# Expert tiles of 96 slots shared in column groups, with two overflow units in a thirteenth tile

## The chip, the cores and the metric

One core of one Trainium2 chip runs the whole program. The metric is the device time of one execution in microseconds; for a kernel it is the median of its runs. Inputs, weights and outputs are float32 in HBM.

## The reference, cut to what matters

The program is one inference step of a decoder of two layers, for 512 prompt tokens and 32 sample tokens (8 sequences of 4). Each layer has a projection, a gated recurrence, differential attention (the sample tokens against a paged cache), an output projection and then a mixture of experts, which alone is changed here:

```python
def hier_moe(xn, w_r1, b_r1, w_r2, b_r2, w_gate, w_up, w_down):
    xt = xn.reshape(-1, d)                                # 544 tokens of width 1024
    ... top-1 group of 4, top-2 of the 4 experts in it, weights from the two softmaxes
    y = jnp.zeros_like(xt)
    for e in range(N_EXPERTS):                            # 16
        h = jax.nn.silu(xt @ w_gate[e]) * (xt @ w_up[e])  # width 512
        y = y + (h * gates[:, e:e + 1]) @ w_down[e]
    return y.reshape(b, t, d)
```

So each token goes to exactly two experts: 1088 assignments over 16 experts in a layer, 68 for an expert on average.

## The kernel before, in words

Everything is written out by hand: each engine has its own list of instructions, in a fixed order, with waits on semaphores between them. A helper `link` on VectorE makes each instruction wait for the one before it.

**Routing.** After the output projection, `logits` (L868) and `route` (L1538) find each token's two experts. A matmul with a triangular matrix counts each assignment's position in its expert. `psel` holds, per token and expert, the slot or −1. An expert has P = 128 slots, which are the 128 rows of its tile.

**One expert, one tile.** For expert e, `sel_build` (L1625) compares the slots with 0..127, `slot_ids` (L878) multiplies that selection with the token number and the gate value, and `ids_out` (L1632) brings both to SBUF. POOL gathers the tokens' rows from HBM by an indirect DMA into `xe` (L1889). `x_turn` (L888) transposes them with eight matmuls against the identity, and VectorE scales them on the way to `xeT` (`x_out`, L1618). `gate_up` (L899) is 2 × 8 matmuls with 128 tokens as the stationary operand and 512 columns of weights moving. ScalarE takes the silu (L1249), VectorE multiplies gate value, silu and up (L1752). `h_turn` (L912) transposes, and `down` (L921) is 2 × 4 matmuls. ScalarE copies the two halves of the result (L1255, L1257) and POOL stores the tile in `y_scratch` (`y_store`, L1831).

**The order on TensorE** (L1017 to L1026) is, for each e: `gate_up(e)`, `x_turn(e+1)`, `down(e-1)`, `slot_ids(e+2)`, `h_turn(e)`. The other engines follow the same order.

**Weights.** SP loads them in the order of `weight_plan` (L122), gate, up and down of each expert, 2 MB each, in six slots of SBUF in turns. `load_w` (L450) waits until the last matmul on the slot's former content is done (`last_use`, L403). Before the experts start, six loads are out.

**Overflow.** Assignments beyond slot 127 of an expert go to extra tiles. `extra_plan` (L1578) counts them and finds each one's expert; after the sixteen tiles, `extra_tiles` (L419) runs as many extra tiles as a register says, all engines in lockstep: the tile's weights are loaded by an address from a register into slots 2, 3 and 4 (L527), then ids, gather, transposes, matmuls and the store follow each other with nothing beside them.

**Results.** `result_rows` (L1600) works out for each token the two rows of `y_scratch` that hold its results. POOL gathers these (L1911) and VectorE adds them to the residual (L1798); the next layer or the final norm follows.

**Column groups.** Some parts of the kernel already use matmuls narrower than 128 columns of the stationary operand. In `sample_chunks` (L577) the 32 sample tokens are the stationary operand, and successive chunks go to output partitions 0, 32, 64 and 96 in turns; `quad_scores` (L664), `quad_values` (L699) and `level` (L797) do the like. `level` for b = 64 (L824) has 64 columns, always at output partitions 0 to 63.

```python
                for c in range(DC):
                    a = 32 * (c % 4)
                    x = mm(o[a:a + NS, :], xT[:, c, S:TOK], w[:, c, :], start=(c < 4), stop=(c >= 4))
```

Of the kernel before, what the change touches and what calls it, by code (L numbers as in the profile page):

```python
# [25 lines left out]
P = 128  # L26
# [12 lines left out]
YROWS = NE * P  # L39
# [3 lines left out]
MAXX = 2 * TOK // P  # L43
AT0 = 8

XV = {"sel": 7, "ids": 10, "x": 12, "all": 13}
# [21 lines left out]
def constants():  # L68
# [3 lines left out]
    for i in range(PT):  # L72
# [20 lines left out]
        "ebase": np.broadcast_to(P * np.arange(NE)[None, :], (P, NE)),  # L93
# [27 lines left out]

def weight_plan():  # L122
    plan = []
    for l in range(L):
        plan += [("in", l, j, (2, 3, 0, 1)[j % 4]) for j in range(7)]
        plan += [("out", l, n, 1 - n) for n in range(2)]
        for e in range(NE):
            for k in range(3):
                plan.append((("gate", "up", "down")[k], l, e, (2, 3, 4, 5, 0, 1)[(3 * e + k) % 6]))
    where, count = {}, [0] * 6  # L130
# [9 lines left out]
def build(nc, t_in, t_out):  # L140
# [4 lines left out]
    with ctx:  # L145
# [28 lines left out]
        def wslot(s):  # L174
            return w_a[:, 4096 * s:4096 * (s + 1)] if s < 4 else h_a[:, 4096 * (s - 4):4096 * (s - 3)]
# [70 lines left out]
        smalls = sb("smalls", 2148)  # L246
# [61 lines left out]
        tg = small("id_and_gate", (NT, NE, 2))  # L308
        rk = small("y_rows_f", (2, NT))
        rki = small("y_rows", (2, NT), U32)  # L310
        idx = small("slot_tokens", (NE,), U32)
        gate = small("slot_gates", (NE,))

        rx = m_a[:, 5144:5160]
        cntx = shaped(m_a[:, 5096:5144], (3, NE))
        ohx = small("extra_expert", (MAXX, NE))
        ohx2 = shaped(m_a[:, 4968:5096], (MAXX, NE))
# [5 lines left out]
        tgx = small("extra_id_and_gate", (NT, 2))  # L323
        xid = small("extra_tokens", (1,), U32)
        xidf = small("extra_tokens_f", (1,))
        xgt = small("extra_gates", (1,))
# [3 lines left out]
        y_d = nc.dram_tensor("y_scratch", [YROWS + MAXX * P, D], F32, kind="Internal").ap()  # L330
# [4 lines left out]
        wl = [sem(f"w_loaded{i}") for i in range(6)]  # L335
        kl = [sem(f"x_tile_then_k_page_loaded{i}") for i in range(NK)]
        vl = [sem(f"v_quad_loaded{i}") for i in range(NV)]
        prep_a, prep_v = sem("lb_exps"), sem("prep_steps")
# [64 lines left out]
        def last_use(key):  # L403

            what, l, j = key
            if what == "in":
                return (tp_ps, 12 * l + PT * (j + 1)) if j < 3 else (fp_ps, 32 * l + 8 * (j - 2))
            if what == "out":
                return wo_ps, 10 * l + 2 * (PT - 1) + j + 1
            if what == "down":  # L410
                return y_ps, 2 * (NE * l + j) + 2
            return gu_ps, 2 * (NE * l + j) + (1 if what == "gate" else 2)
# [6 lines left out]
        def extra_tiles(eng, ready, body):  # L419

            eng.wait_ge(rk_ok, ready)
            n = eng.value_load(nxi[0:1, 0:1], min_val=0, max_val=MAXX)
            with eng.If(0 < n):
                with eng.Fori(0, MAXX) as t:
                    with eng.If(t < n):
                        body(t)

                        eng.sem_inc(passed, 1)

# [8 lines left out]
        def _(sp):  # L438
            with nc.allow_non_contiguous_dma(reason="small parameter columns"):
# [10 lines left out]
                def load_w(n):  # L450
# [32 lines left out]
                for l in range(L):  # L483
# [36 lines left out]
                    for q in range(3 * NE):  # L520
# [6 lines left out]
                    def extra(t):  # L527
                        e = sp.value_load(exi[0:1, bass.ds(t, 1)], min_val=0, max_val=NE - 1)
# [5 lines left out]
                    sp.wait_ge(*last_use(("down", l, NE - 2)))  # L534
# [6 lines left out]
        def _(pe):  # L541
# [336 lines left out]
            def slot_ids(l, e):  # L878

                E_ = l * NE + e  # L880
                pe.wait_ge(sel_ok, E_ + 1)
                if e >= 1:
                    pe.wait_ge(id_ok, E_)
# [4 lines left out]
            def x_turn(l, e):  # L888
                E_ = l * NE + e
                pe.wait_ge(xe_in[e % 2], 16 * (l * (NE // 2) + e // 2 + 1))  # L890
                if E_ >= 1:
                    pe.wait_ge(xe_ok, 2 * E_)
                for j in range(2):
                    for c in range(4):
                        k = 4 * j + c
                        x = tr(bank[j][:, c * P:(c + 1) * P], xe[e % 2][:, k * P:(k + 1) * P], ident)  # L896
                    x.then_inc(xe_ps, 1)

            def gate_up(l, e):  # L899

                E_ = l * NE + e
                pe.wait_ge(xe_ok, 2 * E_ + 2)
                if E_ >= 1:
                    pe.wait_ge(hg_ok, E_)
# [7 lines left out]
            def h_turn(l, e):  # L912
                E_ = l * NE + e
                pe.wait_ge(hg_ok, E_ + 1)
                if E_ >= 1:
                    pe.wait_ge(ht_ok, E_)
# [4 lines left out]
            def down(l, e):  # L921
                E_ = l * NE + e
                pe.wait_ge(ht_ok, E_ + 1)
                wwait(pe, ("down", l, e))
                w = weights(("down", l, e), 4)
                for n in range(2):
                    if E_ >= 1:
                        pe.wait_ge(y_ok, 2 * E_ - 1 + n)
                    for c in range(4):
                        x = mm(bank[5 + n][:, :], hT[e % 2][:, c, :], w[:, c, n * WB:(n + 1) * WB], start=(c == 0), stop=(c == 3))  # L930
# [3 lines left out]
            for l in range(L):  # L934
                if l:
                    pe.wait_ge(y_ok, 2 * NE * l)
# [80 lines left out]
                for e in range(NE):  # L1017
                    gate_up(l, e)
                    if e + 1 < NE:
                        x_turn(l, e + 1)  # L1020
                    if e >= 1:
                        down(l, e - 1)
                    if e + 2 < NE:
                        slot_ids(l, e + 2)
                    h_turn(l, e)
                down(l, NE - 1)  # L1026

                def extra(t):
                    V_, A_ = t * XV["all"], t * XA["y"]
                    pe.wait_ge(xv[l], V_ + XV["sel"])  # L1030
                    for i in range(NT):
                        x = mm(bank[7][:, 0:2], sel[:, i, :], tgx[:, i, :], start=(i == 0), stop=(i == NT - 1))
# [26 lines left out]
                pe.wait_ge(y_ok, 2 * NE * (l + 1))  # L1059
# [4 lines left out]
        def _(act):  # L1064
# [70 lines left out]
            for l in range(L):  # L1135
                norm_roots(2 * l)
                if l == 0:

                    act.wait_ge(prep_v, 1)
                    A(lbe[:, :, :], lbe[:, :, :], ACT.Exp).then_inc(prep_a, 1)  # L1140
                    A(dls[:, :, :], dls[:, :, :], ACT.Exp).then_inc(prep_a, 1)
# [28 lines left out]
                if l == 0:  # L1170

                    act.wait_ge(zero_st, 16 * MAXX)
# [70 lines left out]
                for e in range(NE + 1):  # L1243
                    if e < NE:
                        E_ = l * NE + e
                        act.wait_ge(gu_ps, 2 * E_ + 1)
                        if E_ >= 2:
                            act.wait_ge(hg_ok, E_ - 1)
                        A(silu[e % 2], bank[2][:, :], ACT.Silu).then_inc(si_ok, 1)  # L1249
                    if e >= 1:  # L1250
                        E_ = l * NE + e - 1
                        act.wait_ge(y_ps, 2 * E_ + 1)
                        if E_ >= 2:
                            act.wait_ge(y_st[(e - 1) % 2], 16 * (E_ // 2))
                        A(yt[(e - 1) % 2][:, 0:WB], bank[5][:, :], ACT.Copy).then_inc(y_ok, 1)  # L1255
                        act.wait_ge(y_ps, 2 * E_ + 2)
# [697 lines left out]
```

## Time and profile before

| | us |
|---|---|
| median of 3 runs | 2113.6 (2112.17 to 2118.08) |
| profiled execution, its own time | 2108.49 |
| its span, first to last instruction | 2106.8 |
| stage of the sixteen expert tiles, layer 0 | 630 to 998 |
| the same, layer 1 | 1637 to 2013 |
| extra tile, layer 1 (none in layer 0) | 2014 to 2066 |

The span is what the profile shows; the execution's own time is 1.7 us longer. PE is TensorE's matmuls, PEld its weight loads, DVE is VectorE, ACT ScalarE. A record of TensorE is one pass; a float32 matmul leaves two records, a transpose one. The shape 128*64 128x512 of a record is the stationary operand's rows and columns, then the moving operand. A record's duration is longer than its share of the engine, since records overlap; what counts is the distance between starts. "PEclk" is the granted share of TensorE's full clock.

### The profile page before, as it was taken

How to read it: one execution, taken by the hardware profiler on the slowest of the kernel's cores; microseconds unless marked ns; L12 is line 12 of the kernel's file. 1: busy time of each engine (PE TensorE's matmuls, PEld its weight loads, DVE VectorE, ACT ScalarE, POOL GpSimd, SP SyncE). 2: the span in 40 equal slices, each digit the busy share in tenths (PEclk: the TensorE clock that was granted, in tenths of full speed). 3: DMA queues.
4: the chain of work that ended last, by engine and by line, in shares of the span. 5: the costliest groups of instructions: out<-in, count | busy, mean ns of one | idle time of the engine just before them, and what ended most of it. 6: DMA issues, size and time to landing. Idle time of an engine off the chain costs nothing. (4 is left out here: it accounts for less than half of the span.)

```text
span 2106.8 us, 30190 instructions
## 1 busy us (share of the span) xinstructions
PE 1867.4 (89%) x11372; PEld 1094.4 (52%) x11372; DVE 595.9 (28%) x1635; ACT 505.9 (24%) x1072; POOL 181.6 (9%) x236
## 2 busy tenths in 40 slices
PE   7999989787979999999599998988888899999970
PEld 3467767455454554454245776654544444454430
DVE  3215365421141111110420554553213311111103
ACT  2123246455110111011111332654511011111001
POOL 1000022100000010000200001311000010010002
PEclk9999989999969999999799998999998899999985
DMA  8321059897535989986522104888962389988744
GB/s 283 127 75 42 1 190 308 276 310 279 216 112 179 328 300 328 329 303 238 213 91 72 41 21 137 269 293 284 347 239 103 110 315 331 329 300 327 263 150 147
DMA packets 209281, 453.23 MB, mean 215 GB/s; under 512 B 23217, under 2 KB 23218, under 8 KB 209138
## 3 DMA queue, kind: packets, MB, share of 16 engines
q1 hardware_dynamic: 189986, 383.52, 52.5%
q0 software_dynamic: 19152, 67.77, 8.5%
q8 instruction: 93, 1.52, 0.3%
q14 instruction: 50, 0.41, 0.1%
HBM read 413.89 MB, written 37.36 MB: 214 GB/s over the span
## 5 line engine op out<-in xcount | busy, mean ns | idle before, releaser
L909 PE MATMUL bank<-wslots,heads 128*128 128x512 f32 x768 | 339.0, 598 | 2.7 <-DVE heads L1622 2.7
L620 PE MATMUL bank<-xT,wslots 128*128 128x272 f32 x1024 | 241.8, 393 | 1.5 <-ACT heads L1169 0.8
L909 PEld LDWEIGHTS bank<-wslots,heads 128*128 128x128 f32 x768 | 146.1, 192 | 182.0 <-issue 178.4
L620 PEld LDWEIGHTS bank<-xT,wslots 128*128 128x128 f32 x1024 | 191.6, 190 | 40.7 <-issue 3.2
L661 PE MATMUL bank<-cst,wslots 128*128 128x128 f32 x1024 | 164.3, 287 | 12.9 <-DMA wslots<-in_cache_k 7.5
L574 PE MATMUL bank<-wslots,xT 128*128 128x512 f32 x384 | 169.3, 595 | 0.0
L1752 DVE SCALAR_TENSOR_TENSOR temps<-temps,smalls,bank 128x512 f32<-128x512 f32 x32 | 23.9, 747 | 432.1 <-PE bank L909 432.1
L661 PEld LDWEIGHTS bank<-cst,wslots 128*128 128x128 f32 x1024 | 115.5, 144 | 38.9 <-issue 22.8
L861 PE MATMUL bank<-wslots,xT 128*128 128x512 f32 x256 | 115.1, 610 | 3.8 <-DVE xT L1521 3.8
L574 PEld LDWEIGHTS bank<-wslots,xT 128*128 128x128 f32 x384 | 71.3, 190 | 87.5 <-issue 87.3
L930 PE MATMUL bank<-wslots,temps 128*128 128x512 f32 x256 | 112.7, 593 | 1.5 <-ACT temps L1261 1.5
L909 PE MATMUL bank<-hgrn,heads 128*128 128x512 f32 x256 | 112.7, 593 | 0.1
L930 PE MATMUL bank<-hgrn,temps 128*128 128x512 f32 x256 | 112.5, 592 | 0.0
L1219 ACT ACTIVATE heads<-bank 128x512 f32<-128x512 f32 x128 | 74.9, 595 | 110.1 <-PE bank L661 109.8
L1219 ACT ACTIVATE wslots<-bank 128x512 f32<-128x512 f32 x128 | 75.9, 593 | 96.6 <-PE bank L661 88.3
L1255 ACT ACTIVATE heads<-bank 128x512 f32<-128x512 f32 x32 | 19.1, 597 | 323.2 <-PE bank L930 323.2
L1469 DVE TENSOR_SCALAR_CACHE_REDUCE heads<-bank 128x512 f32<-128x512 f32 x64 | 44.2, 691 | 155.8 <-PE bank L672 132.8
L861 PEld LDWEIGHTS bank<-wslots,xT 128*128 128x128 f32 x256 | 49.6, 196 | 66.5 <-issue 62.3
L711 PE MATMUL bank<-wslots,heads 128*32 128x128 f32 x2048 | 75.1, 292 | 6.9 <-ACT heads L1234 6.9
L711 PEld LDWEIGHTS bank<-wslots,heads 128*32 128x32 f32 x2048 | 60.0, 118 | 36.0 <-ACT heads L1234 21.2
L1249 ACT ACTIVATE temps<-bank 128x512 f32<-128x512 f32 x32 | 19.1, 597 | 238.4 <-PE bank L909 238.4
L930 PEld LDWEIGHTS bank<-wslots,temps 128*128 128x128 f32 x256 | 47.4, 190 | 55.5 <-issue 53.6
(332 smaller groups left out, 2078.4 us busy)
## 6 DMA issues: line engine op xcount, KB each, us to landing
wslots<-in_w_up SPq DMA_DIRECT2D x33, 2048.0 KB, 21.1
wslots<-in_cache_k SPq DMA_DIRECT2D x256, 256.0 KB, 4.4
wslots<-in_cache_v SPq DMA_DIRECT2D x256, 256.0 KB, 4.5
wslots<-in_w_gate SPq DMA_DIRECT2D x17, 2048.0 KB, 16.3
hgrn<-in_w_down SPq DMA_DIRECT2D x17, 2048.0 KB, 10.7
hgrn<-in_w_gate SPq DMA_DIRECT2D x16, 2048.0 KB, 16.5
wslots<-in_w_down SPq DMA_DIRECT2D x16, 2048.0 KB, 10.6
wslots<-in_w_in SPq DMA_DIRECT2D x14, 2048.0 KB, 10.0
```

Of the source, the lines that this page charges most:

```text
L574: x = mm(bank[2 + m % 2][:, :], xT[:, c, tok(i)], w[:, c, :], start=(c == 0), stop=(c == DC - 1))
L620: x = mm(bank[6 + g % 2][:, 0:HALF], w[:, c, h * P:(h + 1) * P], xT[:, c, half * HALF:(half + 1) * HALF], start=(c == 0), stop=(c == DC - 1))
L661: x = tr(bank[s % 2][:, h * P:(h + 1) * P], kpage[s % NK][:, h, :], ident)
L711: x = mm(bank[5][32 * h:32 * h + 32, 0:HD], ptq[par][:, j, 32 * h:32 * h + 32], vquad[v % NV][:, j, h, :], start=(q == 0 and j == 0), stop ...
L861: x = mm(bank[2 + s][:, :], oT[:, c, tok(i)], w[:, c, :], start=(c == 0), stop=(c == DC - 1))
L909: x = mm(bank[2 + k][:, :], xeT[e % 2][:, c, :], w[:, c, :], start=(c == 0), stop=(c == DC - 1))
L930: x = mm(bank[5 + n][:, :], hT[e % 2][:, c, :], w[:, c, n * WB:(n + 1) * WB], start=(c == 0), stop=(c == 3))
L1219: A(ktb[s // 4 % 2][:, s % 4].rearrange("p h n -> p (h n)"), bank[s % 2][:, :], ACT.Copy).then_inc(kt_ok, 1)
L1249: A(silu[e % 2], bank[2][:, :], ACT.Silu).then_inc(si_ok, 1)
L1255: A(yt[(e - 1) % 2][:, 0:WB], bank[5][:, :], ACT.Copy).then_inc(y_ok, 1)
L1469: tell(V.tensor_scalar(scr[G_ % 6], bank[2][:, :], 1.0, None, ALU.mult, ALU.max, accum_out=mx5[:, g % 4:g % 4 + 1]), sq_ok)
L1752: link(V.scalar_tensor_tensor(hgt, silu[e % 2], gate[:, e:e + 1], bank[3][:, :], ALU.mult, ALU.mult), hg_ok)
```

## The change

Each expert has 96 slots instead of 128, so four experts share three tiles of 128 rows. The rows of a tile that belong to different experts are multiplied with different weights: a chunk of `gate_up` or `down` is now two or three matmuls, each with 32 or 64 columns of the stationary operand and its own output partitions. Assignments beyond slot 95 form units of 64 rows. The first two units of a layer have a thirteenth tile, whose weights SP loads by register after the others; further units would go through the serial loop. The gate value is no longer multiplied into the tile but when the results are added. The weights have a seventh slot in `xT`.

```diff
-YROWS = NE * P
+CAP, XCAP = 96, 64
+TILES = NE * CAP // P + 1
+YROWS = NE * CAP
-MAXX = 2 * TOK // P
+MAXX = 15
+ZT = 8
...
+def tile_parts(t):
+    if t == TILES - 1:
+        return [(NE, 0, XCAP), (NE + 1, XCAP, P)]
+    parts = []
+    for e in range(NE):
+        lo, hi = max(CAP * e - P * t, 0), min(CAP * (e + 1) - P * t, P)
+        while lo < hi:
+            z = min(hi, lo + 64 if lo % 64 == 0 and hi - lo >= 64 else lo + 32)
+            parts.append((e, lo, z))
+            lo = z
+    return parts
+
+def tiles_of(e):
+    return [t for t in range(TILES) if any(e == x for x, _, _ in tile_parts(t))]
 def weight_plan():
+    need = []
+    for e in range(NE + 2):
+        t = tiles_of(e)
+        need += [(3 * t[0], e, "gate", 3 * t[-1]), (3 * t[0] + 1, e, "up", 3 * t[-1] + 1), (3 * t[0] + 5, e, "down", 3 * t[-1] + 5)]
+    need.sort(key=lambda x: x[:2])
...
-        for e in range(NE):
-            for k in range(3):
-                plan.append((("gate", "up", "down")[k], l, e, (2, 3, 4, 5, 0, 1)[(3 * e + k) % 6]))
+        free = {s: k - 7 for k, s in enumerate((2, 3, 4, 5, 0, 1, 6))}
+        for _, e, what, last in need:
+            slot = min(free, key=lambda s: free[s])
+            free[slot] = last
+            plan.append((what, l, e, slot))
...
+                    elif j >= NE:
+                        sp.wait_ge(rk_ok, l + 1)
+                        e = sp.value_load(exi[0:1, j - NE:j - NE + 1], min_val=0, max_val=NE - 1)
+                        src = t_in["w_" + what][l, bass.ds(e, 1)].rearrange("o k n -> (o k) n")
...
-                    for q in range(3 * NE):
+                    for q in range(3 * (NE + 2)):
+                        if q == 6:
+                            sp.wait_ge(lg_ps, NT * (l + 1))
...
-                    x = mm(bank[7][:, 0:2], sels[e % 2][:, i, :], tg[:, i, e, :], start=(i == 0), stop=(i == NT - 1))
+                    x = mm(bank[7][:, 0:1], sels[T_ % 2][:, i, :], tokid[:, i:i + 1], start=(i == 0), stop=(i == NT - 1))
...
+                parts = tile_parts(t)
                 for k, what in enumerate(("gate", "up")):
-                    wwait(pe, (what, l, e))
-                    w = weights((what, l, e), DC)
+                    for e, _, _ in parts:
+                        wwait(pe, (what, l, e))
                     for c in range(DC):
-                        x = mm(bank[2 + k][:, :], xeT[e % 2][:, c, :], w[:, c, :], start=(c == 0), stop=(c == DC - 1))
+                        for e, a, z in parts:
+                            x = mm(bank[2 + k][a:z, :], xeT[T_ % 2][:, c, a:z], weights((what, l, e), DC)[:, c, :], start=(c == 0), stop=(c == DC - 1))
                     x.then_inc(gu_ps, 1)
...
                     for c in range(4):
-                        x = mm(bank[5 + n][:, :], hT[e % 2][:, c, :], w[:, c, n * WB:(n + 1) * WB], start=(c == 0), stop=(c == 3))
+                        for e, a, z in parts:
+                            x = mm(bank[5 + n][a:z, :], hT[T_ % 2][:, c, a:z], weights(("down", l, e), 4)[:, c, n * WB:(n + 1) * WB],
+                                   start=(c == 0), stop=(c == 3))
...
-                b16 = lambda a: a.unsqueeze(2).to_broadcast([P, NT, NE])
-                t16 = r16.rearrange("p i g j -> p i (g j)")
-                link(V.tensor_tensor(t16, f1, b16(r1[:, 6]), ALU.mult))
-                link(V.tensor_tensor(psel[:, :, :], f2, b16(r1[:, 7]), ALU.mult))
-                V.tensor_copy(tg[:, :, :, 0], b16(con("tokid")))
-                link(V.tensor_tensor(tg[:, :, :, 1], t16, psel[:, :, :], ALU.add))
...
-                link(V.tensor_scalar(cntx[:, 0], cnt, float(P), None, ALU.is_gt))
-                for k in range(2, NT):
-                    link(V.scalar_tensor_tensor(cntx[:, 0], cnt, float(P * k), cntx[:, 0], ALU.is_gt, ALU.add))
+                link(V.tensor_scalar(cntx[:, 0], cnt, float(CAP), None, ALU.is_gt))
+                for k in range(1, -(-(TOK - CAP) // XCAP)):
+                    link(V.scalar_tensor_tensor(cntx[:, 0], cnt, float(CAP + XCAP * k), cntx[:, 0], ALU.is_gt, ALU.add))
...
-                link(V.tensor_tensor(sels[e % 2], iota.unsqueeze(1).to_broadcast([P, NT, P]), psel[:, :, e].unsqueeze(2).to_broadcast([P, NT, P]),
-                                ALU.is_equal), sel_ok)
+                for e in range(NE):
+                    base = CAP * e - P * t
+                    lo, hi = max(base, 0), min(base + CAP, P)
+                    if lo < hi:
+                        x = V.scalar_tensor_tensor(dst[:, :, lo:hi], iota[:, lo:hi].unsqueeze(1).to_broadcast([P, NT, hi - lo]), float(-base),
+                                                   psel[:, :, e].unsqueeze(2).to_broadcast([P, NT, hi - lo]), ALU.add, ALU.is_equal)
+                link(x, sel_ok)
...
-                V.tensor_copy(idx[:, e:e + 1], bank[7][:, 0:1])
-                link(V.tensor_copy(gate[:, e:e + 1], bank[7][:, 1:2]), id_ok)
+                link(V.tensor_copy(idx[:, t:t + 1], bank[7][:, 0:1]), id_ok)
...
-                    link(V.scalar_tensor_tensor(hgt, silu[e % 2], gate[:, e:e + 1], bank[3][:, :], ALU.mult, ALU.mult), hg_ok)
+                    link(V.tensor_tensor(hgt, silu[T_ % 2], bank[3][:, :], ALU.mult), hg_ok)
...
-                        link(V.tensor_tensor(hid[0:r, i, :], hid[0:r, i, :], yg[2 * i + k][0:r, :], ALU.add), moe_add)
+                        link(V.scalar_tensor_tensor(hid[0:r, i, :], yg[2 * i + k][0:r, :], r1[0:r, 6 + k, i:i + 1], hid[0:r, i, :], ALU.mult, ALU.add), moe_add)
```

The parts of the tiles are, in turns: 64 and 32 columns of one expert and 32 of the next; 64 of one and 64 of the next; 32 of one and 32 and 64 of the next. The thirteenth tile is 64 of unit 0 and 64 of unit 1. For this tile `sel_build` first works out the slots of the two units with three small operations each. The loops over experts on POOL, ScalarE and VectorE run over the thirteen tiles in the same order as before, and `extra_tiles` counts from the third unit.

## Rows read from the trace of the kernel before

**Rows 1.** The page, part 1: busy us, share of the span, instructions.
```profile
PE 1867.4 (89%) x11372; PEld 1094.4 (52%) x11372; DVE 595.9 (28%) x1635; ACT 505.9 (24%) x1072; POOL 181.6 (9%) x236
```

**Rows 2.** Windows: stretch, length, busy PE, PEld, DVE, ACT, POOL, clock, DMA share, GB/s.
```profile
630.00:998.00 368.00, 367.15 (x1092) 180.99 (x1092) 51.79 (x110) 37.39 (x63) 25.63 (x29) 0.99 0.79 285
1637.00:2013.00 376.00, 370.83 (x1108) 183.99 (x1108) 59.26 (x137) 37.46 (x64) 27.70 (x31) 0.98 0.79 282
...
694.70:704.70 10.00, 10.00 (x27) 4.50 (x25) 0.89 (x2) 1.19 (x2) 1.45 (x2) 1.00 0.96 344
704.70:714.70 10.00, 10.00 (x31) 4.93 (x30) 2.13 (x3) 0.60 (x1) 0.00 (x0) 1.00 1.03 385
```

**Rows 3.** Timeline (start, us, engine, line), one expert of layer 0: TensorE, then SP.
```profile
694.76 7.03 PE L909 MATMUL bank<-hgrn,heads 128*128 128x512 f32 x16
701.63 7.03 PE L909 MATMUL bank<-wslots,heads 128*128 128x512 f32 x16
...
693.45 0.37 SPq L463 DMA_DIRECT2D wslots<-in_w_down  x1
...
716.43 0.37 SPq L463 DMA_DIRECT2D hgrn<-in_w_down  x1
```

**Rows 4.** Timeline of POOL after the last expert tile, layer 0, then layer 1.
```profile
999.50 0.53 POOL L1834 DMA_DIRECT2D y_scratch<-heads  x1 [7.45 <-ACT heads L1257]
1003.22 0.98 POOL L1911 DMA_INDIRECT hgrn<-y_scratch,smalls  x1 [3.20 <-DMA y_scratch<-heads]
...
2013.98 0.53 POOL L1834 DMA_DIRECT2D y_scratch<-heads  x1 [7.90 <-ACT heads L1257]
...
2065.84 0.99 POOL L1911 DMA_INDIRECT hgrn<-y_scratch,smalls  x1 [6.62 <-issue]
```

**Rows 5.** DMA issues: count, KB each, median us from issue to landing.
```profile
wslots<-in_w_up SPq DMA_DIRECT2D x33, 2048.0 KB, 21.1
...
y_scratch<-heads POOLq DMA_DIRECT2D x33, 512.0 KB, 8.7
```

**Rows 6.** Timeline of TensorE in short windows: the 32-wide matmuls of L581.
```profile
45.38 1.07 PE L581 MATMUL bank<-wslots,xT 128*32 128x512 f32 x8
...
45.84 1.04 PE L581 MATMUL bank<-wslots,xT 128*32 128x512 f32 x8
...
46.70 0.61 PE L581 MATMUL bank<-wslots,xT 128*32 128x512 f32 x4
47.24 1.13 PE L574 MATMUL bank<-wslots,xT 128*128 128x512 f32 x2
```

**Rows 7.** The same: from 32-wide to 32-wide work, and from 32-wide to 64-wide.
```profile
300.76 1.07 PE L672 MATMUL bank<-heads,smalls 128*32 128x512 f32 x8
301.65 0.19 PE L818 MATMUL bank<-hgrn 128*32 128x32 f32 x1
...
332.46 1.06 PE L672 MATMUL bank<-heads,smalls 128*32 128x512 f32 x8
333.45 0.27 PE L824 MATMUL bank<-hgrn 128*64 128x64 f32 x1
```

**Rows 8.** Two lines' matmuls: duration ns min/median/max, first and last start.
```profile
L581 PE MATMUL bank<-wslots,xT x160: 592/592/617, 45.4 to 1592.4; 128*32 128x512 f32 x160
...
L824 PE MATMUL bank<-hgrn x64: 222/222/271, 333.5 to 1353.2; 128*64 128x64 f32 x64
```

**Rows 9.** Timeline of VectorE ahead of the first expert tile, layer 0.
```profile
624.48 0.59 DVE L1583 SCALAR_TENSOR_TENSOR temps<-bank,temps 128x16 f32<-128x16 f32 x3
...
625.54 0.29 DVE L1588 TENSOR_TENSOR smalls<-cst,temps 128x128 f32<-128x128 f32 x1
...
628.62 1.42 DVE L1622 TENSOR_TENSOR heads<-bank,smalls 128x512 f32<-128x512 f32 x2
```

**Rows 10.** Groups of VectorE by form: busy us, mean ns, idle before them.
```profile
L1752 DVE SCALAR_TENSOR_TENSOR temps<-temps,smalls,bank 128x512 f32<-128x512 f32 x32 | 23.9, 747 | 432.1 <-PE bank L909 432.1
...
L1803 DVE SCALAR_TENSOR_TENSOR hid<-hid,smalls,xT 128x1024 f32<-128x1024 f32 x4 | 5.1, 1284 | 0.1
```

More of the change, by code:

```diff
@@ L42 @@
 HALF = TOK // 2
-MAXX = 2 * TOK // P
+MAXX = 15
+ZT = 8
 AT0 = 8
-XV = {"sel": 7, "ids": 10, "x": 12, "all": 13}
+XV = {"sel": 4, "ids": 5, "x": 7, "all": 8}
 XP = {"ids": 1, "x": 2, "gate_up": 3, "h": 4, "all": 5}
@@ L307, in build @@
         psel = small("slot_or_none", (NT, NE))
[L308 removed]
         rk = small("y_rows_f", (2, NT))
         rki = small("y_rows", (2, NT), U32)
[L311 to L315, printed above, removed]
+        idx = small("slot_tokens", (TILES,), U32)
+        rx = m_a[:, 5272:5288]
+        cntx = shaped(m_a[:, 5224:5272], (3, NE))
         ohx = small("extra_expert", (MAXX, NE))
[L317 removed]
+        ohx2 = shaped(m_a[:, 4968:4968 + MAXX * NE], (MAXX, NE))
         kx = small("extra_first_slot", (MAXX,))
@@ L409, in last_use @@
                 return wo_ps, 10 * l + 2 * (PT - 1) + j + 1
+            t = TILES * l + tiles_of(j)[-1]
             if what == "down":
-                return y_ps, 2 * (NE * l + j) + 2
-            return gu_ps, 2 * (NE * l + j) + (1 if what == "gate" else 2)
+                return y_ps, 2 * t + 2
+            return gu_ps, 2 * t + (1 if what == "gate" else 2)
         def projected(l, n):
@@ L919, in h_turn, with down @@
                 x.then_inc(ht_ps, 1)
[L921 to L925, printed above, removed]
+            def down(l, t):
+                T_ = l * TILES + t
+                pe.wait_ge(ht_ok, T_ + 1)
+                parts = tile_parts(t)
+                for e, _, _ in parts:
+                    wwait(pe, ("down", l, e))
                 for n in range(2):
-                    if E_ >= 1:
-                        pe.wait_ge(y_ok, 2 * E_ - 1 + n)
+                    if T_ >= 1:
+                        pe.wait_ge(y_ok, 2 * T_ - 1 + n)
                     for c in range(4):
-                        x = mm(bank[5 + n][:, :], hT[e % 2][:, c, :], w[:, c, n * WB:(n + 1) * WB], start=(c == 0), stop=(c == 3))
+                        for e, a, z in parts:
+                            x = mm(bank[5 + n][a:z, :], hT[T_ % 2][:, c, a:z], weights(("down", l, e), 4)[:, c, n * WB:(n + 1) * WB],
+                                   start=(c == 0), stop=(c == 3))
                     x.then_inc(y_ps, 1)
@@ L1016, in _ @@
                 x_turn(l, 0)
[L1017 to L1026, printed above, removed]
+                for t in range(TILES):
+                    gate_up(l, t)
+                    if t + 1 < TILES:
+                        x_turn(l, t + 1)
+                    if t >= 1:
+                        down(l, t - 1)
+                    if t + 2 < TILES:
+                        slot_ids(l, t + 2)
+                    h_turn(l, t)
+                down(l, TILES - 1)
                 def extra(t):
@@ new lines, in sel_build @@
+            def sel_build(l, t):
+                T_ = l * TILES + t
+                if T_ >= 2:
+                    dve.wait_ge(id_ps, T_ - 1)
+                dst = sels[T_ % 2]
+                if t == TILES - 1:
+                    for u in range(2):
+                        extra_slots(ohx[:, u:u + 1, :].to_broadcast([P, NT, NE]), kx[:, u:u + 1].to_broadcast([P, NT]))
+                        x = V.tensor_tensor(dst[:, :, XCAP * u:XCAP * (u + 1)], iota[:, 0:XCAP].unsqueeze(1).to_broadcast([P, NT, XCAP]),
+                                            psx[:, :].unsqueeze(2).to_broadcast([P, NT, XCAP]), ALU.is_equal)
+                        if u == 0:
+                            link(x)
+                    link(x, sel_ok)
+                    return
+                for e in range(NE):
[4 more added lines that the diff above has]
+                                                   psel[:, :, e].unsqueeze(2).to_broadcast([P, NT, hi - lo]), ALU.add, ALU.is_equal)
+                link(x, sel_ok)
```

231 lines of the change are left out of this document (114 added, 117 removed).

## The prediction

> **What bounds the kernel now.** I first took the page: TensorE is busy 1867 of 2107 us [rows 1]. The windows over the two expert stages say more: 367 of 368 us busy in layer 0, 371 of 376 in layer 1, at a granted clock of 0.99 and 0.98 [rows 2]. So the expert stage is bounded by what TensorE issues, and its time can be counted. The timeline of one expert gives the count [rows 3]: gate, up and down are 24 matmuls, and a float32 matmul leaves two records, so 48; 16 of them take from 694.76 to 701.63, 0.429 us each, 20.6 us in all. Eight transposes, the slot ids and four transposes fill up the rest of the period, which SP's issues of the down weights measure (693.45, 716.43). One expert costs **22.98 us**.
>
> The second bound is near. Over the stage the DMA engines are 0.79 busy at 285 GB/s; in the first 20 us of an expert's period they run saturated, at 344 and 385 GB/s, and then they are done [rows 2]. Third, after the loop layer 1 runs one overflow tile alone: from the last store of a normal tile to the first gather of results it takes 51.86 us, in layer 0 3.72 us [rows 4]. The tile costs **48.1 us**, all of it serial.
>
> How many tiles are needed comes from the inputs. I counted the router's choices in the reference on its drawn inputs: the two fullest experts have 112 and 103 tokens in layer 0, 132 and 103 in layer 1, all others 91 or fewer. With 128 slots that is one overflow, in layer 1, and the profile agrees (33 stores of result tiles, one more than 2 × 16 [rows 5]). With 96 slots it is two units of 64 in each layer: the thirteenth tile holds them and no serial tile is left.
>
> **The change, part by part (per layer unless said).**
>
> (a) 16 tiles become 13: −3 × 22.98 = −68.9 us.
>
> (b) The twelve shared tiles are no longer one matmul 128 wide per chunk. Tile_parts cuts them, in turns, into 64+32+32, 64+64 and 32+32+64 columns; the thirteenth is 64+64. What parts of one width cost is shown: eight 32-wide matmuls (16 records) start in fours at 45.38, 45.84, 46.27 and 46.70 (the first, second and last of these starts stand in [rows 6]), so four column groups run together at the pace of one full matmul. What a change of width costs is shown too. After a quad of 32-wide records the next 32-wide work starts 0.89 us after the quads began, the next 64-wide work 0.99 us after (300.76 to 301.65, 332.46 to 333.45), and to full width it is 46.70 to 47.24, 0.54 instead of 0.43 [rows 6, 7]. Each change of width costs 0.10 us (0.99 − 0.89) after the stream has ended, whether it goes from 32 to 64 or to 128, and the first record behind it is 25 ns longer at width 32 (617 against 592) and 49 ns at width 64 (271 against 222) [rows 8], as its weights were not loaded beneath the stream before.
>
> That in these rows everything before the change has ended is the point on which all hangs: there the column groups overlap anyway. In a mixed tile they don't, and no row shows a 64-wide matmul in groups 0–1 beside a 32-wide one in group 2. I take it that a change of width waits for the whole array, because the gap is the same whatever widths and groups are involved, and because the weights of the next width aren't preloaded as those of the same width are. The Trainium skill (TensorEngine Tiling (Array Packing), Key Properties) says so outright: changing the tiling mode, "not just tile", drains the engine; 128×64 and 128×32 are separate modes there. Another page of the Trainium skill (TensorE: Matmul & The Clock Gate, Packing small matmuls) has matmuls at different tile positions run together and would make a mixed chunk as cheap as a pure one; that is the first rival below.
>
> So a mixed chunk is: 64-wide part, two records, 0.858; change 0.10 + 0.025; the 32-wide parts together, 0.858; change back 0.10 + 0.049. Sum 1.99 us where a full chunk costs 0.858, +1.132 us. A tile has 8 + 8 + 4 + 4 = 24 chunks, and 8 of the 13 tiles are mixed: 24 × 8 × 1.132 = **+217.3 us**. The five pure tiles stay at 24 × 0.858. Bounds: with changes that cost nothing 1.716 a chunk (+164.7); with the dearest change seen, into full width (0.10, and 0.105 on the first record behind it: 47.24 with 1.13 for two records, so the second 0.54 behind the first, less the record's own 0.59 [rows 6]), 2.126 a chunk (+243.5).
>
> (c) Each tile's column matmuls also lie between full-width transposes: two ways in and two out, at about 0.14 us each; the mixed tiles' ways in are counted in (b). 5 × 4 + 8 × 2 = 36 changes, +5.0 us. Between 0 and 7.
>
> (d) VectorE ahead of the first tile. TensorE waits there for L1622, which stands behind the plan of the overflow tiles (L1581 to L1598) [rows 9]. The plan gains three comparisons (0.59 us for three) and seven operations go from 128 to 240 columns (0.29 us for 128 against about 0.17 for the 16 of L1583, so 112 columns more are +0.12): +1.4 us. Two selection matrices, built by two instructions each instead of one: +0.3. The dropped gate values (four operations) lay under the wait for slot positions. +1.7 us, exposed; between 1 and 2.5.
>
> (e) At nothing: the selection of the last tile (eight small VectorE operations) and the split ones, since VectorE idles 432 us ahead of L1752 [rows 10]; their cover is the tile period. The gate moves from L1752 to the last additions, two-operand becoming three-operand at 1.28 us as L1803 is [rows 10]: some 0.05 us each for ten, partly behind the gathers. Three stores and three gathers fewer on POOL, never waited for. SP: six loads more per layer, 12.6 MB, behind a wait for the plan; the plan is done some 6 us after L1622 begins (628.62), and those loads are the last of the layer. The seventh slot, in xT, waits for the logits, over before the plan begins; the six loads ahead of it are issued before the stage as now. 18 × 6.29 MB of weights and 13 × 1.05 MB of rows are 127 MB in over 500 us, 245 GB/s, less than now. If (b) is wrong that cover is gone: see the rival.
>
> (f) The serial tile: −48.1 us, once.
>
> Sum: 2 × (−68.9 + 217.3 + 5.0 + 1.7) − 48.1 = **+262 us**. The profiled execution took 2108.5 us (span 2106.8), so 2370.6; the median of the three runs shown lies 5.1 us higher, so **2375 us**. Bounds of this case, on the median 2113.6: 2 × (−68.9 + 164.7 + 0 + 1) − 48.1 = +145.5, or 2259, and 2 × (−68.9 + 243.5 + 7 + 2.5) − 48.1 = +320, or 2434.
>
> **Rivals.**
> *Disjoint groups don't wait for each other (faster).* Place: the second part of a mixed chunk, in tile 0 the 32-wide matmul in columns 64 to 95 behind the 64-wide one. If it starts a few ns after it, as the quads of [rows 6] do, every tile costs 24 × 0.858 and each layer −68.9 + 13 × 4 × 0.14 + 1.7 = −59.9, so 2113.6 − 119.8 − 48.1 = 1946 by TensorE alone. Then the loads come last: 127 MB less the 12.6 loaded before are 114 MB, at 365 GB/s (between 344 and 385 [rows 2]) 313 us, against 306 us of matmuls; at the pace of weights now, 6.29 MB in the 21.1 us to the landing of the up weights, the last of an expert's three [rows 5], 298 GB/s, 338 us. A gain of 18 to 60 us per layer, I take 35: 2 × (−35) − 48 = −118, **1995 us** (1950 to 2040). The sign turns where a mixed chunk costs 1.31 us: (68.9 + 24.1 − 1.7 − 5.0) / 192 = 0.45 above 0.858. For it: queues of single groups plainly exist, since records of four groups overlap although each matmul's two stand together. Against it: the constant gap.
> *Two 64-wide halves don't overlap either.* No row has a second half in columns 64 to 127. Five tiles would take 20.6 us more each: +206, **2581 us**. Little speaks for it, as four quarters overlap.
> *The change doesn't do what it says.* A third overflow unit in a layer would bring back a serial tile at 48 us: **2423 us**. The counts exclude it for these inputs, unless rounding moves several tokens.
>
> **How the numbers follow.** The forecast gets 0.80, the fast rival 0.15, the halves 0.03, a third unit 0.01, a sum that happens to end near now 0.01. The range 2255 to 2435 is the bounds of the forecast, and takes in the third unit; 0.19 is left out. Both signs don't share the chance evenly, so it is not widened to 1950. About 0.3%, 6 us, is what a measurement tells from no change: faster 0.15, same 0.01, slower 0.84.
>
> **What would show it.** In the changed profile, gate and up of a mixed tile take about 31.8 us and down 15.9, of a pure tile 13.7 and 6.9, with the periods in a pattern of long, short, long. In a mixed chunk the records start in steps of 0.48, 0.53, 0.45 and 0.53 us. TensorE never waits for weights, DMA throughput in the stage falls below 285 GB/s, each stage lasts some 520 us, and the first gather follows the last store by 4 us in both layers. It is wrong if records of width 64 and 32 start within 0.05 us of each other; if TensorE waits for wslots; or if a pure tile is as long as a mixed one.

## The result, and the profile after

The changed kernel takes **2374.4 us** (median of 4 runs, 2371.5 to 2375.3) against 2115.8 for the kernel before: ratio 1.122, 95% interval 1.121 to 1.124, or +258.6 us. Forecast were +262 us and 2375.

The page of the changed kernel, part 1, answers to [rows 1]: busy us, share, instructions. TensorE is 281 us busier, and nothing else grew.

```profile
PE 2148.6 (91%) x12898; PEld 974.4 (41%) x12898; DVE 576.8 (24%) x1596; ACT 489.7 (21%) x1044; POOL 168.4 (7%) x222
```

Its windows over the two stages of thirteen tiles answer to [rows 2] (same columns):

```profile
635.00:1155.00 520.00, 518.90 (x1890) 125.99 (x1890) 43.24 (x98) 30.42 (x51) 19.67 (x23) 1.00 0.60 217
1803.00:2326.00 523.00, 519.70 (x1892) 125.99 (x1890) 45.41 (x103) 30.57 (x52) 19.64 (x23) 0.99 0.59 212
```

Still one engine without a gap, now for 520 us instead of 368, at an undiminished clock, while the DMA engines fell from 0.79 to 0.60 busy. TensorE's list of waits has no weight transfer in it. So the time lies in what TensorE does, and its timeline shows where: tile 0's up (mixed), the pure tile 1, and the mixed chunks of tile 0's `down` (start, us, engine, line).

```profile
652.68 15.95 PE L949 MATMUL bank<-hgrn,heads 128*64 128x512 f32 x48
668.56 1.09 PE L934 MATMUL bank<-cst,heads 128*128 128x128 f32 x8
...
671.10 7.09 PE L949 MATMUL bank<-wslots,heads 128*64 128x512 f32 x32
678.01 0.59 PE L949 MATMUL bank<-hgrn,heads 128*64 128x512 f32 x1
678.02 0.59 PE L949 MATMUL bank<-wslots,heads 128*64 128x512 f32 x1
678.44 0.59 PE L949 MATMUL bank<-hgrn,heads 128*64 128x512 f32 x1
678.45 0.59 PE L949 MATMUL bank<-wslots,heads 128*64 128x512 f32 x1
...
686.00 1.62 PE L973 MATMUL bank<-xT,temps 128*64 128x512 f32 x3
687.01 0.62 PE L973 MATMUL bank<-wslots,temps 128*32 128x512 f32 x1
687.46 0.59 PE L973 MATMUL bank<-xT,temps 128*32 128x512 f32 x1
687.47 0.59 PE L973 MATMUL bank<-wslots,temps 128*32 128x512 f32 x1
687.99 1.62 PE L973 MATMUL bank<-xT,temps 128*64 128x512 f32 x3
```

Up of the mixed tile takes 15.9 us (652.68 to 668.56), gate of the pure tile 6.9 (671.10 to 678.01). In the pure tile the two halves start 10 ns apart. In the mixed one a chunk repeats every 1.99 us (686.00, 687.99): the 64-wide matmul (two records in the first group of three), then 1.01 us after its first record the two 32-wide ones, side by side, then the next 64-wide one 0.98 us later. The 32-wide matmuls have column groups of their own, 64 to 95 and 96 to 127, and still don't start before the other stream has ended.

POOL behind the last tile of each layer, against [rows 4]:

```profile
1156.17 0.53 POOL L1888 DMA_DIRECT2D y_scratch<-heads  x1 [7.81 <-ACT heads L1301]
1159.95 0.98 POOL L1965 DMA_INDIRECT hgrn<-y_scratch,smalls  x1 [3.25 <-DMA y_scratch<-heads]
...
2326.74 0.53 POOL L1888 DMA_DIRECT2D y_scratch<-heads  x1 [7.81 <-ACT heads L1301]
2332.33 0.98 POOL L1965 DMA_INDIRECT hgrn<-y_scratch,smalls  x1 [5.06 <-DMA y_scratch<-heads]
```

No serial tile is left in layer 1: 5.6 us instead of 51.9. To compare kernels without what varies outside the changed part, I take from each trace the stretch between the first counting matmul of the router (L1001, now L1045) and the first gather of results, in both layers:

| us | layer 0 | layer 1 |
|---|---|---|
| before | 613.66 to 1003.22: 389.56 | 1628.33 to 2065.84: 437.51 |
| after | 617.58 to 1159.95: 542.37 | 1788.00 to 2332.33: 544.33 |
| difference | +152.8 | +106.8 |
| by the prediction's steps | −68.9 + 217.3 + 5.0 + 1.7 = +155.1 | 155.1 − 48.1 = +107.0 |

These two give 259.6 of the 266.9 us by which the profiled span grew. The other 7.3 lie outside: 3.9 ahead of the first counting matmul, 2.9 between the layers, 0.4 at the end.

### The profile page after: what moved, and what is told of

It reads as the page before. It is cut to its first block and busy times, and to the rows that moved or that the text cites. A ratio compares the mean times of both kernels' runs of the same rounds, so it can differ in the third digit from the quotient of the medians.

```text
span 2373.7 us, 33022 instructions
## 1 busy us (share of the span) xinstructions
PE 2148.6 (91%) x12898; PEld 974.4 (41%) x12898; DVE 576.8 (24%) x1596; ACT 489.7 (21%) x1044; POOL 168.4 (7%) x222
## 5 line engine op out<-in xcount | busy, mean ns | idle before, releaser
L949 PE MATMUL bank<-wslots,heads 128*64 128x512 f32 (+1 forms) x1280 | 479.4, 608 | 5.2 <-DVE heads L1659 5.2
L949 PE MATMUL bank<-hgrn,heads 128*64 128x512 f32 (+1 forms) x608 | 278.8, 604 | 0.0
L973 PE MATMUL bank<-wslots,temps 128*64 128x512 f32 (+1 forms) x608 | 263.7, 606 | 0.0
L949 PEld LDWEIGHTS bank<-wslots,heads 128*64 128x64 f32 (+1 forms) x1280 | 98.3, 123 | 308.1 <-issue 301.8
L949 PE MATMUL bank<-xT,heads 128*64 128x512 f32 (+1 forms) x288 | 140.6, 607 | 0.0
L973 PE MATMUL bank<-hgrn,temps 128*64 128x512 f32 (+1 forms) x288 | 137.7, 599 | 1.4 <-ACT temps L1304 1.4
L612 PEld LDWEIGHTS bank<-wslots,xT 128*128 128x128 f32 x384 | 73.5, 196 | 90.9 <-issue 90.6
L973 PEld LDWEIGHTS bank<-wslots,temps 128*64 128x64 f32 (+1 forms) x608 | 52.0, 122 | 131.7 <-issue 131.7
L949 PEld LDWEIGHTS bank<-hgrn,heads 128*64 128x64 f32 (+1 forms) x608 | 55.7, 122 | 113.3 <-issue 113.3
L973 PE MATMUL bank<-xT,temps 128*64 128x512 f32 (+1 forms) x192 | 95.7, 611 | 0.0
```

Source lines behind the costliest of these rows:

```text
L612: x = mm(bank[2 + m % 2][:, :], xT[:, c, tok(i)], w[:, c, :], start=(c == 0), stop=(c == DC - 1))
L949: x = mm(bank[2 + k][a:z, :], xeT[T_ % 2][:, c, a:z], weights((what, l, e), DC)[:, c, :], start=(c == 0), stop=(c == DC - 1))
L973: x = mm(bank[5 + n][a:z, :], hT[T_ % 2][:, c, a:z], weights(("down", l, e), 4)[:, c, n * WB:(n + 1) * WB], start=(c == 0), stop=(c == 3))
```

## The experiments

My theory: a change of width waits for the whole array, so a mixed chunk is two streams and two changes. Rivals: it is the number of small matmuls, or the reading of different weight tiles, or each change itself, with the parts still overlapping.

**All shared tiles in 32-wide parts.** `tile_parts` alone:

```diff
-            z = min(hi, lo + 64 if lo % 64 == 0 and hi - lo >= 64 else lo + 32)
+            z = min(hi, lo + 32)
```

> The changed kernel with every shared tile cut into four parts of 32 columns, so that no tile mixes widths (the thirteenth stays 64+64). Theory (a change of width waits for the whole array; parts of one width overlap): a chunk of a mixed tile falls from 1.99 to 0.86 us, TensorE alone would give 2374 - 2 x 217 = 1940 us; the loads come next, 114 MB per layer after the stage's start, so 1940 to 2030 us, and TensorE then waits for wslots or hgrn weights. Rival 1 (the cost is in the number of matmuls and of weight loads, not in their widths): the records rise from 64 x 2 to 96 x 2 in a mixed tile, so slower than 2374 us. Rival 2 (two matmuls of one tile from different weights don't overlap): no gain, about 2374.

Measured: **1957.6 us**, ratio to before 0.925 (0.923 to 0.926). More matmuls than the changed kernel, the same bytes, and 417 us less. The parts of a chunk that read different weight tiles run side by side, up of one expert beside up of another:

```profile
656.90 0.60 PE L949 MATMUL bank<-hgrn,heads 128*32 128x512 f32 x2
656.91 0.60 PE L949 MATMUL bank<-wslots,heads 128*32 128x512 f32 x2
657.33 0.60 PE L949 MATMUL bank<-hgrn,heads 128*32 128x512 f32 x2
657.34 0.60 PE L949 MATMUL bank<-wslots,heads 128*32 128x512 f32 x2
```

Neither the count nor the different weights is the cost. The windows of this kernel show the second bound coming close (same columns as above):

```profile
633.00:943.00 310.00, 306.45 (x2658) 108.74 (x2650) 42.18 (x94) 30.60 (x52) 19.52 (x23) 0.99 0.98 365
1596.00:1908.00 312.00, 306.11 (x2654) 108.38 (x2646) 41.57 (x91) 30.54 (x52) 19.50 (x23) 0.99 0.95 356
```

The DMA engines are 0.98 and 0.95 busy at 365 and 356 GB/s, yet TensorE waits little for weights, 4.8 + 2.5 + 0.9 = 8.2 us over both layers by its list of waits:

```profile
PE bank L949 <- DMA hgrn<-in_w_up: 4.8, 4, 2.1
PE bank L949 <- DMA wslots<-in_w_up: 2.5, 2, 2.3
PE bank L973 <- DMA wslots<-in_w_down: 0.9, 1, 0.9
```

**The same parts, sorted by width.** All 64-wide parts of a gate, up or down half first, then the 32-wide ones; the matmuls are the changed kernel's, only their order differs.

```diff
+def by_width(parts, chunks):
+    return [(c, p) for w in (64, 32) for c in range(chunks) for p in parts if p[2] - p[1] == w]
...
-                    for c in range(DC):
-                        for e, a, z in parts:
+                    for c, (e, a, z) in by_width(parts, DC):
```

> The changed kernel with the same matmuls in another order: in gate, up and each half of down first the 64-wide parts of all chunks, then the 32-wide ones. Theory: the 0.858 us of a second stream per chunk stay, the 0.27 us of two changes per chunk fall to eight changes per mixed tile: 2 x (192 x 0.274 - 64 x 0.137) = 88 us less, 2287 us. Rival (all of a mixed chunk's 1.13 us is the change itself, two at 0.57 us, and the parts would overlap otherwise): 2 x (217 - 36) less, about 2010 us. Rival (no cost of order at all): 2374.

Measured: **2287.6 us** (ratio 1.081, 1.079 to 1.083), 86.8 below the changed kernel. One half of a `down` in this kernel:

```profile
679.13 4.20 PE L975 MATMUL bank<-xT,temps 128*64 128x512 f32 x9
682.71 0.62 PE L975 MATMUL bank<-wslots,temps 128*32 128x512 f32 x1
...
686.26 4.20 PE L975 MATMUL bank<-xT,temps 128*64 128x512 f32 x9
```

The 64-wide stream lasts 3.58 us, the 32-wide one 3.55. Eight records at 0.429 are 3.43, so a change costs 0.15 and 0.12 us, the 0.149 and 0.125 of the prediction. With nearly all changes gone the two streams still follow each other. So of the 1.13 us extra in a mixed chunk about a quarter is the changes, three quarters the overlap that is lost.

**Two halves in every shared tile.** Each tile is multiplied as two 64-wide halves with the weights of its first and last expert.

```diff
+def halves(t):
+    parts = tile_parts(t)
+    return [(parts[0][0], 0, 64), (parts[-1][0], 64, P)]
...
-                        for e, a, z in parts:
+                        for e, a, z in halves(t):
```

In each mixed tile the 32 rows of the second expert within a half get the wrong expert's weights; all loads stay.

> The changed kernel with every shared tile multiplied as two halves of 64 columns, the first with the weights of the tile's first expert, the second with those of its last; the rows that belong to another expert get the wrong weights, all loads and waits stay. Theory: as the tiles of four 32-wide parts, 1940 to 2030 us, since one width is as good as another. If four quarters cost anything beyond two halves (issue, weight loads), this one is faster than they are by that.

Measured: **1954.5 us** (ratio 0.924, 0.921 to 0.925), as the all-32 kernel within the spread of both. One width per tile is what counts, not which.

**The kernel before without its serial tile.** The count of extra tiles is multiplied by zero, so that layer 1 leaves out the few assignments beyond slot 127.

```diff
-                link(V.tensor_copy(nxi[:, :], cntx[:, 1, NE - 1:NE]))
+                link(V.tensor_scalar(nxi[:, :], cntx[:, 1, NE - 1:NE], 0.0, None, ALU.mult))
```

> The kernel before with the count of overflow tiles set to zero: the few assignments beyond slot 127 of one expert in layer 1 are left out. Theory: the serial tile costs 48.1 us, so 2068 us. Rival (part of it lies beside the next steps' work, such as loads that wait anyway): a difference of 30 to 45 us.

Measured: **2072.2 us**, ratio 0.979 (0.978 to 0.981), 45.1 us less. POOL at the end of layer 1:

```profile
2019.52 0.53 POOL L1834 DMA_DIRECT2D y_scratch<-heads  x1 [7.90 <-ACT heads L1257]
2024.82 0.98 POOL L1911 DMA_INDIRECT hgrn<-y_scratch,smalls  x1 [4.77 <-DMA y_scratch<-heads]
```

The gather follows the store by 5.3 us here, not by the 3.7 of layer 0. The tile is 51.86 − 5.30 = 46.6 us by the traces. The medians can't part this from the rival (30 to 45 us), since their ratio allows 40 to 47 us; by the traces nearly the whole tile was serial, as the theory has it.

**The cut alone, in the kernel before.** Three kernels cut the gate of each expert and leave all else, with the same weights for all 128 columns. The first:

```diff
-                        x = mm(bank[2 + k][:, :], xeT[e % 2][:, c, :], w[:, c, :], start=(c == 0), stop=(c == DC - 1))
+                        for a, z in ((0, 64), (64, 96), (96, 128)) if k == 0 else ((0, 128),):
+                            x = mm(bank[2 + k][a:z, :], xeT[e % 2][:, c, a:z], w[:, c, :], start=(c == 0), stop=(c == DC - 1))
```

> The kernel before, all else as it is (same weights for all 128 columns, one change): each of the 8 gate chunks of the sixteen shared experts is cut into matmuls 64, 32 and 32 columns wide. Theory (a change of width waits for the whole array, 1.132 us more per mixed chunk): 256 chunks x 1.132 = +290 us, and 32 ways out to full width at 0.10 + 0.105 = +7, so about 2412 us; a gate of 8 chunks lasts about 15.9 us instead of 6.87. Rival (the mixed chunks of the changed kernel are dear because their parts read different weight tiles): the cut by itself costs only its ways in and out, about 2126 us.

The second has `((0, 32), (32, 64), (64, 96), (96, 128))` in the place of the three parts:

> The kernel before, each gate chunk cut into four matmuls 32 columns wide, same weights. Theory (only a change of width costs): one way in at 0.125 and one out at 0.205 us per expert, 32 x 0.33 = +11 us, about 2126 us. Rival (narrow matmuls cost by their number, so that the 0.62 us by which a tile of the all-32 kernel is longer than a full one is 24 chunks at 0.026 us): 256 x 0.026 = +7 us, 2122 us. Rival (three more matmuls per chunk are what makes mixed chunks dear): as dear as the kernel with 64, 32 and 32, or dearer, over 2400 us.

The third alternates, so that every chunk is one stream but the width changes from chunk to chunk:

```diff
+                        wide = (128, 64 if c % 2 == 0 else 32)[k == 0]
+                        for a in range(0, 128, wide):
+                            x = mm(bank[2 + k][a:a + wide, :], xeT[e % 2][:, c, a:a + wide], w[:, c, :], start=(c == 0), stop=(c == DC - 1))
```

> The kernel before, gate chunks cut 64 + 64 where c is even and 4 x 32 where it is odd, same weights: eight changes of width and one way out per gate, but every chunk one stream. Theory (a change costs 0.10 us and an exposed weight load; the rest of a mixed chunk's 1.132 us is a second stream of 0.858): 4 changes to 64 at 0.149, 4 to 32 at 0.125, one to full width at 0.205, 1.30 us per expert, +42 us, about 2157 us. Rival (the parts of a mixed chunk do overlap and each change itself costs half of 1.132 us): 9 x 0.566 x 32 = +163 us, about 2279 us.

Measured, beside 2117.6 for the kernel before:

| | us | ratio, 95% | stretch, layer 0 | per expert more than before |
|---|---|---|---|---|
| 64+32+32 | 2407.6 | 1.134 to 1.140 | 536.29 | 146.7 / 16 = 9.17 |
| 4 × 32 | 2123.6 | 1.001 to 1.005 | 394.37 | 4.8 / 16 = 0.30 |
| alternating | 2155.9 | 1.015 to 1.021 | 410.45 | 20.9 / 16 = 1.31 |

TensorE's timeline of one expert shows the gate and behind it the up at full width; first 64 + 32 + 32:

```profile
722.47 15.95 PE L910 MATMUL bank<-hgrn,heads 128*64 128x512 f32 x48
738.35 7.13 PE L910 MATMUL bank<-wslots,heads 128*128 128x512 f32 x16
```

4 × 32:

```profile
700.74 7.07 PE L910 MATMUL bank<-hgrn,heads 128*32 128x512 f32 x64
707.74 7.13 PE L910 MATMUL bank<-wslots,heads 128*128 128x512 f32 x16
```

and alternating:

```profile
702.84 8.09 PE L911 MATMUL bank<-hgrn,heads 128*64 128x512 f32 x48
710.86 7.13 PE L911 MATMUL bank<-wslots,heads 128*128 128x512 f32 x16
```

A gate takes 15.88, 7.00 and 8.02 us where it took 6.87 [rows 3]. Counted with the ways in and out, the second gate has 2 changes of width and loses 0.3 us, the alternating one 9 and loses 1.3, the mixed one 17 and loses 9.2. The first two agree on some 0.15 us per change; at that price 17 changes are 2.5 us, and only a second stream in each of the eight chunks (8 × 0.858 = 6.9) accounts for the rest. The predicted sums per expert were 8 × 1.132 + 0.205 = 9.26, 0.33 and 1.30 us. For the second kernel the medians don't part the theory (2126 us) from the cost by number (2122); the timeline does: by number the gate alone would be 8 × 0.026 = 0.21 us longer, but it is 0.13 longer, and the up behind it, which has not been cut, takes 7.13 us instead of 7.03, as after a change to full width. With no other part of the change present, this settles that the cost is the mixing of widths.

**The first tile's rows ahead of the plan.** What is left in the all-32 kernel is the wait of the first gate for L1659, which stands behind the plan of the overflow tiles.

```diff
-                extra_plan(l)
                 x_out(l, 0)
+                extra_plan(l)
```

> The changed kernel with all shared tiles in 32-wide parts, and on VectorE the copies of the first tile's transposed rows (L1620) ahead of the plan of the overflow tiles. In the all-32 kernel the first gate of a layer waits 2 and 2.9 us for that copy (L949 <- heads L1659; the 5.5 us of the first is the larger). Theory (the plan stands in front of the first tile): about 5 us less than the all-32 kernel's 1957.6, 1952 us. Rival (the rows themselves come late, or the second tile then waits for the plan): no change.

The next keeps this (its expectation calls the kernel above e8), with the four 64 + 64 tiles left as they are:

```diff
-            z = min(hi, lo + 64 if lo % 64 == 0 and hi - lo >= 64 else lo + 32)
+            z = min(hi, lo + (64 if t % 3 == 1 else 32))
```

> As e8, but the tiles that are 64 + 64 (4 of 12) are left 64 wide, the others in 32-wide parts. Each tile still has one width, so by the theory the time is that of e8 within 3 us, about 1952 us: a way in to 64 costs 0.149 instead of 0.125 us, half as many matmuls are issued. Rival (the number of matmuls matters, or 64-wide halves run faster than quarters as the 1954.5 us of the halves kernel might be read): 1 to 3 us less than e8.

Measured: 1958.9 us (ratio 0.923 to 0.927) and **1953.6 us** (0.922 to 0.926). The first brings no gain over the 1957.6, although the wait went from 2.88 to 0.85 us. The windows show a part of why, the all-32 kernel first (last columns: granted clock, DMA share, GB/s):

```profile
632.00:634.00 2.00, 1.80 (x12) 0.49 (x16) 1.73 (x9) 0.00 (x0) 0.00 (x0) 0.50 0.00 0
634.00:636.00 2.00, 2.00 (x20) 0.54 (x16) 1.73 (x9) 0.00 (x0) 0.00 (x0) 0.73 0.00 0
636.00:638.00 2.00, 2.00 (x24) 0.55 (x20) 1.79 (x8) 0.00 (x0) 0.00 (x0) 1.00 0.00 0
```

and then with the rows ahead of the plan:

```profile
631.00:633.00 2.00, 1.58 (x8) 0.40 (x12) 1.73 (x9) 0.00 (x0) 0.00 (x0) 0.50 0.00 0
633.00:635.00 2.00, 2.00 (x16) 0.56 (x12) 1.83 (x6) 0.00 (x0) 0.00 (x0) 0.50 0.01 4
635.00:637.00 2.00, 2.00 (x20) 0.47 (x16) 1.77 (x7) 0.00 (x0) 0.00 (x0) 0.67 0.00 0
```

TensorE's timeline of the same kernel, the first gate and the beginning of up:

```profile
631.42 9.48 PE L949 MATMUL bank<-wslots,heads 128*32 128x512 f32 x64 [0.85 <-DVE heads L1659]
640.73 4.46 PE L949 MATMUL bank<-hgrn,heads 128*32 128x512 f32 x40
```

Behind the waits of the routing TensorE is granted 0.50 (1.2 of 2.4 GHz), and in these windows the clock rises during the first gate. The gate begins 1.92 us earlier behind the first counting matmul (15.91 instead of 17.83), but runs longer at half clock, 9.31 us to the start of up instead of 8.31: 0.92 of 1.92 us are left. Later in the stages TensorE's waits for up weights grew from 7.3 to 10.5 us, which I read as weights that arrive no earlier, since the transfers are nearly at their own pace; no run tests this. The stretch is 333.04 and 337.13 us against 333.20 and 337.64. The second kernel waits 7.7 us for weights and has 332.00 and 334.36. Whether that is its wider tiles or chance is open, as the intervals overlap. It is the fastest kernel here that leaves out no part of the work, 160 us below the one before; the all-32 kernel, whose only edit to the changed kernel is one line, is as good within the spread.

## Why the prediction was right, point by point

- **(b) the mixed chunk**, 1.99 us, is what decided it, and all its parts were measured: 1.99 in the changed kernel, 15.88 / 8 = 1.985 with only the gate cut, 0.149 and 0.125 for the changes by the sorted kernel. The record starts foretold as 0.48, 0.53, 0.45, 0.53 came as 1.01 for the first two together, 0.45 and 0.53. That [rows 6, 7] show the gap only where groups overlapped anyway was the weak point of the argument; the constant gap carried it.
- The rule of the Trainium skill (TensorEngine Tiling (Array Packing), Key Properties), that a change of tiling mode drains the engine, holds here: 1.01 us from a 64-wide matmul to a 32-wide one in other columns, 10 ns between two 64-wide ones. The other page of the Trainium skill (TensorE: Matmul & The Clock Gate, Packing small matmuls), which has matmuls at different tile positions run together, agrees with the traces for parts of one width alone: the four 32-wide ones of the all-32 kernel start 10 ns apart, in pairs, the 32-wide ones of a mixed chunk 1.01 us behind the 64-wide one.
- **(a), (b), (c)** can be checked together in the repeating tiles: three in a row (two mixed, one pure) take 124.36 us, between the `h_turn` transposes (L958) at 703.02, 827.38, 951.73 and 1076.09 us. The prediction's terms give 3 × 22.98 + 48 × 1.132 + 8 × 0.14 = 124.4. The periods of the single tiles there are 41.5, 50.4 and 32.5 us, and not simply long, short, long, since `down` of one tile lies in the period of the next.
- **All of (a) to (d)** gave +152.8 us in layer 0 where 155.1 was forecast. About 1.1 us of the 2.3 lies in the first tile: from its first gate to its `h_turn` it is 17.2 us longer than before (17.95 and 35.12 us), where two times 8 mixed chunks and a way out make 18.3. Most of that goes with the clock, which both kernels have at 0.50 when the first gate starts: gate and up take 16.04 us there instead of 2 × 6.87 in the kernel before (2.3 us lost), and 33.15 instead of 2 × 15.88 in the changed one (1.4 us lost), where the granted clock is 0.91 from 638 to 640 us and 1.00 behind. The prediction had no term for this.
- **(d)** can be read alone: 16.43 us from the first counting matmul to the first gate became 17.83 (635.41 − 617.58), +1.40 for a forecast of 1.7. Ahead of the plan nothing was lost (10.61 us from the first counting matmul to its first instruction before, 10.56 after), so the 0.3 for the two-part selections was not paid; the plan, from there to the rows' copy, went from 4.35 to 5.80 us, +1.45 for 1.4.
- **(f) the serial tile** was mis-sized: 48.1 forecast, 46.6 by the traces, 45.1 by the medians. I subtracted layer 0's 3.72 us from store to gather; in layer 1 without the tile it is 5.3 (5.6 in the changed kernel). In layer 1 this and the 1.7 us by which (a) to (d) were forecast too high there cancel: +106.8 against +107.0.
- **(e)** held where it was checked: no wait for weights, DMA at 217 and 212 GB/s. The 245 GB/s of the prediction was too high by its own terms: it divides all 127 MB by the stage, though 12.6 MB of them are loaded before it; 114 MB in 520 us are 219. And what SP's last loads wait for is the end of `result_rows` (`rk_ok`, L1653 of the changed kernel); the plan itself is done before the rows' copy begins. The additions with the gate went from 1225 to 1285 ns each, as forecast.
- The mechanism was right, but that the median was hit within 1 us is partly luck: between the profiled executions the difference is 266.9 us, of which 7.3 lie outside what was changed, and between the medians 258.6; the steps gave 262. The forecast was set on a median of 2113.6, and the kernel before was measured 2.2 us above that, which hides most of the 3.4 us by which the difference was too large.
- **The rivals.** *Disjoint groups don't wait* is refuted by the timeline. Its price can be tested, since the all-32 kernel is what it described: 1957.6 us, at the fast end of its 1950 to 2040. Its step that failed is the pace of the loads: I took a gain of 35 us per layer, halfway between the two load rates; the stretch of layer 0 shrank by 56.4. The loads run at 365 GB/s, and the 298 GB/s worked out from issue to landing I now read as the pace of loads that lie one behind the other in a queue, not that of the transfers; this reading is not tested. *Two halves don't overlap* is refuted by the pure tiles. *A third unit* didn't occur.

## What to carry to other kernels

Column groups of TensorE work side by side only among matmuls of one width. Where matmuls of two widths alternate, each width is a stream of its own, and the gain from packing is gone before any price of the change; cut all parts to the smallest width instead. Four 32-wide matmuls cost what one full matmul does here, so the finer cut was free and turned 12% loss into 7.5% gain. And before a start is moved earlier, look at the granted clock there: work that begins at half clock gives back part of the gain.

## What the runs showed of the hardware that was not expected

**The clock after a gap differs from one profiled run to the next, with the same code there.** Between the layers, where neither theory nor change has anything, TensorE idles for 26.5 to 27.4 us, transposes, and starts the projections. The same 16 matmuls (32 records) took 14.00 us in the kernel before and 16.71 in the changed kernel, which explains 2.7 of the 2.9 us found there. The windows of before:

```profile
1035.50:1049.50 14.00, 14.00 (x36) 6.28 (x35) 1.15 (x5) 0.60 (x1) 0.00 (x0) 1.00 0.16 58
```

and of after:

```profile
1192.60:1197.00 4.40, 4.40 (x7) 1.85 (x6) 0.29 (x1) 0.00 (x0) 0.00 (x0) 0.50 0.35 128
1197.00:1209.30 12.30, 12.30 (x29) 5.44 (x28) 0.85 (x4) 0.60 (x1) 0.00 (x0) 0.95 0.00 0
```

With before's own code there they took 15.96 us (64+32+32 in the gate) and 15.59 us (4 × 32), so it is not the change. I take such starts to be a part of the few us by which single runs of one kernel differ, but each kernel was profiled only once, so that is not shown. A forecast from one profiled run carries them.

**The transfers can keep the DMA engines 0.98 busy over 310 us** (365 GB/s) with TensorE nearly never waiting. 0.79 busy at 285 GB/s [rows 2] was not close to a bound, but paced by TensorE.
